# Ten norms of a float32 transformer kernel: the sum of squares as a rounded high and low part

## The chip, the cores and the metric

The kernel runs on one core of a Trainium2 chip. The metric is the device time of one execution in microseconds (us). TensorE is PE in the profile, VectorE is DVE, ScalarE is ACT, GpSimd is POOL. Before the change three runs took 3339.12 to 3342.34 us, with a median of 3340.39 us.

## What is computed

Two blocks of layers, in float32, on 512 tokens of width 1024: feed-forward parts (`swiglu`), mixers (a gated MLP with retention, multi-head attention over latents, a gated linear recurrence) and cross attention to a memory. What matters here is the norm in front of each of them:

```python
def rms_norm(x, g):
    xf = x.astype(jnp.float32)
    y = xf * lax.rsqrt(jnp.mean(xf * xf, axis=-1, keepdims=True) + RMS_EPS)
    return (y * g).astype(x.dtype)
```

The mean of `x*x` over the 1024 features of a token is the sum that the change is about.

## The kernel before

x is held transposed: eight tiles of 128 features by 512 tokens. A product with a weight in near float32 precision is made of three products of rounded parts (type fp32r): high weight by high input, high by low, low by high. A weight unit is 128x1024 (eight tiles of 128x128), so that most units are 24 products of 128x512. There are 588 units; SyncE streams them, ScalarE rounds each to its high part (`whi`, L818), GpSimd subtracts to get the low part (`wlo`, L2182), and TensorE uses them in a fixed order (`unit`, L334 to L346, whose products are L341, L342 and L345).

The work is a chain of twelve stages, 0 to 11: feed-forward at 0, 2, 3, 5, 8 and 11, first mixer at 1 and 4, second mixer at 6, cross attention at 7 and 10, third mixer at 9. A stage ends with `residual`: for each of the eight output tiles m, VectorE adds the product's bank to x (L1472), ScalarE squares x (L849) and rounds x times the gain to `gxh` (L851), VectorE writes the rest to `gxl` (L1480) and adds the square to `acc` (L1483). So `acc`, 128x512, holds the sum of squares over the tiles, and what is left is a sum over the 128 partitions.

That sum is `norm(i)` (L385, by `total`, L381): one matmul of a 128x128 matrix of ones with `acc`, in full float32 precision, into bank 7. In the first product of stage i, TensorE goes through the eight tiles as they arrive; the norm comes right behind this first unit. The gains are in the products' inputs, and the factor 1/rms is only applied behind the products: ScalarE takes the square root (L826, `root`), VectorE the reciprocal (L1359, `rstd`, into R), and VectorE multiplies the banks by R. At stage 9 the unit is taken apart: `high` (16 products), then the norm, then `low` (8 products). Stages 0, 6 and the last norm have orders of their own.

Each engine works through its list in order. On VectorE the last instructions of a residual are, for tile 7, `gxl` and then `acc`; behind them comes the reciprocal of the next stage, which waits for ScalarE. On ScalarE the order there is `gxh`, then the rounding of a weight unit (L818), then the root. On GpSimd there is only the subtraction of the weight units, each as soon as its `whi` is there.

Of the kernel before, what the change touches and what calls it, by code (L numbers as in the profile page):

```python
# [6 lines left out]
F32 = mybir.dt.float32  # L7
F32R = mybir.dt.float32r
I32 = mybir.dt.int32
ALU = mybir.AluOpType  # L10
# [3 lines left out]
P = 128  # L14
SEQ = 512
D = 1024
KD = D // P
# [30 lines left out]
M2_STAGE = 6  # L48
XA_STAGE = (7, 10)
M3_STAGE = 9  # L50
F_SCALE = (0.5, 0.5, 0.5, 0.5, 1.0, 1.0)


# [90 lines left out]
class Signals:  # L144


    def __init__(self, nc, ctx, known):
        self.nc, self.ctx, self.known = nc, ctx, known
        self.handles, self.counts, self.values = {}, {}, {}
# [16 lines left out]
class Memory:  # L166


    def __init__(self, nc, ctx):
        self.nc = nc  # L170
        self.stack = ctx
        sb = self.sb
        self.x = sb("x", KD * SEQ)
        self.gxh, self.gxl = sb("gxh", KD * SEQ, F32R), sb("gxl", KD * SEQ, F32R)
        self.raw = [sb(f"raw{r}", UNIT) for r in range(SLOTS)]
        self.whi = [sb(f"whi{r}", UNIT, F32R) for r in range(SLOTS)]
        self.wlo = [sb(f"wlo{r}", UNIT, F32R) for r in range(SLOTS)]
        self.R, self.acc = sb("R", SEQ), sb("acc", SEQ)
        self.sq, self.xs, self.sd = sb("sq", SEQ), sb("xs", SEQ), sb("sd", SEQ)
        self.ones, self.ident = sb("ones", P, side="right"), sb("ident", P, side="right")  # L180
        self.epsilons, self.later = sb("epsilons", P, side="right"), sb("later", P, side="right")
        self.lcols = [sb(f"lcol{l}", LCOL["all"], side="right") for l in range(DEPTH)]
        self.rcol = sb("rcol", RCOL["all"], side="right")
        self.blocks, self.causal = sb("blocks", P, side="right"), sb("causal", P, side="right")
        self.bank = [ctx.enter_context(nc.psum_tensor(f"bank{n}", [P, 512], F32)) for n in range(8)]
        self.f = [self.ffn_tiles(f) for f in range(6)]
        self.squares = [self.acc, self.sq, self.xs, self.sd, self.R, self.f[0]["a"], self.f[0]["s"], self.f[0]["u"]]
        self.m1 = [self.mixer1_tiles(l) for l in range(DEPTH)]
        self.m2 = self.mixer2_tiles()
        self.xa = [self.memory_tiles(a) for a in range(2)]  # L190
        self.m3 = self.mixer3_tiles()

    def sb(self, name, cols, dt=F32, side="left"):
        return self.stack.enter_context(self.nc.sbuf_tensor(name, [P, cols], dt, side=side))
# [107 lines left out]
def tensor_program(pe, S, M):  # L302
# [78 lines left out]
    def total(emptied, of, n=SEQ):  # L381
        b = claim(7, *emptied)
        return pe.matmul(b[:, 0:n], M.ones[:, :], of, start=True, stop=True)  # L383

    def norm(i):  # L385
        pe.wait_ge(*S.at("acc", i - 1, KD - 1))
        total(("root", i), M.acc[:, :]).then_inc(*S.tick("sum", i))

# [353 lines left out]
    def mixer3():  # L742
# [21 lines left out]
        b = next_bank("xp", 0)  # L764
        high(("m3x", 0), b[:, :], [("gx", M3_STAGE - 1, k) for k in range(KD)])
        norm(M3_STAGE)
        low(("m3x", 0), b[:, :])
# [16 lines left out]
        for m in range(X_EARLY):  # L784
            banks.append(next_bank("xs", M3_STAGE, m))
            part(("o3", m), banks[m][:, :], pairs, range(0, 6), True, False, arrive if m == 0 else None)
        for m in range(X_EARLY):
            part(("o3", m), banks[m][:, :], pairs, range(6, KD), False, True, arrive if m == 0 else None)
        for m in range(X_EARLY, KD):
            unit(("o3", m), next_bank("xs", M3_STAGE, m)[:, :], pairs)  # L790

# [16 lines left out]
def scalar_program(act, S, M, T_in):  # L808
# [11 lines left out]
    def ahead(key):  # L820
        split_hi(U[key] + AHEAD)
# [6 lines left out]
    def residual(i, keys):  # L828
        per, gain = len(keys) // KD, gain_after(M, i)
        if i == M3_STAGE - 1:  # L830
            act.wait_ge(*S.at("hidden", 4, KF - 1))
# [4 lines left out]
        for m in range(KD):  # L836
            for j in range(per):
                if keys[m * per + j]:
                    ahead(keys[m * per + j])
            if i == M3_STAGE - 1 and m == 2:  # L840
                act.wait_ge(*S.at("lam", "ready"))
# [509 lines left out]
def vector_program(dve, S, M):  # L1351
# [9 lines left out]
    def used(*key):  # L1361
        return S.at("used", U[key])
# [77 lines left out]
    def residual(i, last, scale):  # L1440
        gain = gain_after(M, i)
        dve.wait_ge(*(S.at("y2", KD - 1) if i == M2_STAGE else S.at("sum", i)))
        dve.memset(M.acc[:, :], 0.0).then_inc(*S.tick("acc", i, -1))
        if i == M2_STAGE - 1:
            dve.wait_ge(*S.at("hidden", 3, KF - 1))
            dve.memset(M.R[:, :], 0.0).then_inc(*S.tick("acc2", -1))
        for m in range(KD):
            if i == M2_STAGE and m:
                scale_x(m)
            if i == M2_STAGE - 1 and m == 1:  # L1450
                rope_angles()
            if i == M3_STAGE - 1 and m == 1:
                decay_bounds()
            if i == M3_STAGE - 1 and m == 3:
                decay_rates()
            if i == M3_STAGE - 1 and m == 4:
                reset_positions()
            if i == M2_STAGE - 1 and m == 4:
                dve.wait_ge(*S.at("sin", "rsin"))
                dve.tensor_scalar(M.m2["rsin"][:, :], M.m2["rsin"][:, :], M.rc("sign"), None, ALU.mult).then_inc(  # L1460
                    *S.tick("rope_table"))
            dve.wait_ge(*used(*last(m)))
            dve.wait_ge(*S.at("acc", i, m - 1))
            if i == M2_STAGE - 1:
                dve.wait_ge(*S.at("acc2", m - 1))
            if i == M2_STAGE:
                dve.wait_ge(*S.at("x_scaled", m))
            elif i:
                dve.wait_ge(*S.at("xs", i - 1, m))
            else:  # L1470
                dve.wait_ge(*S.at(f"x_tile{m}"))
            dve.scalar_tensor_tensor(seq(M.x, m), at_bank("xs", i, m)[:, :], scale, seq(M.x, m), ALU.mult,  # L1472
                                     ALU.add).then_inc(*S.tick("xs", i, m))
            if i == F_STAGE[5]:
                if m < KD - 1:
                    dve.wait_ge(*S.at("sq", i, m))
                    dve.tensor_tensor(M.acc[:, :], M.acc[:, :], M.sq[:, :], ALU.add).then_inc(*S.tick("acc", i, m))
                continue
            dve.wait_ge(*S.at("gxh", i, m))
            dve.scalar_tensor_tensor(seq(M.gxl, m), seq(M.x, m), gain(m), seq(M.gxh, m).bitcast(F32), ALU.mult,  # L1480
                                     ALU.subtract).then_inc(*S.tick("gx", i, m))
            dve.wait_ge(*S.at("sq", i, m))
            dve.tensor_tensor(M.acc[:, :], M.acc[:, :], M.sq[:, :], ALU.add).then_inc(*S.tick("acc", i, m))  # L1483
            if i == M2_STAGE - 1:
                dve.wait_ge(*S.at("acc2", m - 1))
                dve.wait_ge(*S.at("sq2", m))
                dve.tensor_tensor(M.R[:, :], M.R[:, :], M.sd[:, :], ALU.add).then_inc(*S.tick("acc2", m))
# [14 lines left out]
    def ffn(f):  # L1502
        i, T = F_STAGE[f], M.f[f]
        for m in range(KF):
# [8 lines left out]
            if m:  # L1513
# [9 lines left out]
                *S.tick("hidden", f, m))  # L1523
        residual(i, lambda m: ("down", f, m, 2), F_SCALE[f])

# [635 lines left out]


def pool_program(pool, S, M):
    for name, t in (("ones", M.ones), ("blocks", M.blocks), ("causal", M.causal)):
        pool.memset(t[:, :], 1.0).then_inc(*S.tick("fill", name))
    pool.memset(M.ident[:, :], 0.0).then_inc(*S.tick("fill", "ident"))
    pool.wait_ge(*S.at("fill", "ident"))
    pool.affine_select(out=M.ident[:, :], in_=M.ident[:, :], compare_op=ALU.not_equal, fill=1.0, base=0,
                       pattern=[[-1, P]], channel_multiplier=1).then_inc(*S.tick("masks", "ident"))
    pool.memset(M.epsilons[:, :], EPS).then_inc(*S.tick("fill", "epsilons"))  # L2170
    pool.memset(M.later[:, :], 0.0).then_inc(*S.tick("fill", "later"))
    pool.wait_ge(*S.at("fill", "later"))
    pool.affine_select(out=M.later[:, :], in_=M.later[:, :], compare_op=ALU.is_ge, fill=NEG, base=0,
                       pattern=[[-1, P]], channel_multiplier=1).then_inc(*S.tick("masks", "later"))
    pool.affine_select(out=M.causal[:, :], in_=M.causal[:, :], compare_op=ALU.is_ge, fill=0.0, base=0,
                       pattern=[[1, P]], channel_multiplier=-1).then_inc(*S.tick("masks", "causal"))
    for u in range(NU):
        if u in BY_VECTOR:
            continue
        r = u % SLOTS  # L2180
        pool.wait_ge(*S.at("hi", u))
        pool.tensor_tensor(M.wlo[r][:, :], M.raw[r][:, :], M.whi[r][:, :].bitcast(F32), ALU.subtract).then_inc(  # L2182
            *S.tick("lo", u))
# [157 lines left out]
```

## Time and profile before

| | us |
|---|---|
| median of three runs | 3340.39 |
| the profiled execution | 3341.62 |
| its span | 3340.3 |
| TensorE busy in matmuls | 3268.9 (98%) |
| VectorE busy | 1586.5 (47%) |
| GpSimd busy | 1412.4 (42%) |
| ScalarE busy | 1034.6 (31%) |

The span runs from the first to the last instruction of the program; 1.3 us of the execution lie around it. The profile has a page for the whole execution, and views: a timeline (instructions in order, with the idle time before each and what ended it), the groups by line, the source view of one line, and windows (busy time of each engine in a stretch, and the clock that TensorE was granted, as a share of 2.4 GHz). The ends of matmuls are modelled, so that neighbouring ones overlap in the timeline; how fast TensorE goes is read from start to start. A float32 matmul shows as two MATMUL records, so one norm is two rows of L383, which the timeline may merge into one with x2.

### The profile page before, as it was taken

How to read it: one execution, taken by the hardware profiler on the slowest of the kernel's cores; microseconds unless marked ns; L12 is line 12 of the kernel's file. 1: busy time of each engine (PE TensorE's matmuls, PEld its weight loads, DVE VectorE, ACT ScalarE, POOL GpSimd, SP SyncE). 2: the span in 40 equal slices, each digit the busy share in tenths (PEclk: the TensorE clock that was granted, in tenths of full speed). 3: DMA queues.
4: the chain of work that ended last, by engine and by line, in shares of the span. 5: the costliest groups of instructions: out<-in, count | busy, mean ns of one | idle time of the engine just before them, and what ended most of it. 6: DMA issues, size and time to landing. Idle time of an engine off the chain costs nothing.

```text
span 3340.3 us, 36010 instructions
## 1 busy us (share of the span) xinstructions
PE 3268.9 (98%) x14666; PEld 2673.8 (80%) x14666; DVE 1586.5 (47%) x1826; ACT 1034.6 (31%) x1336; POOL 1412.4 (42%) x583
## 2 busy tenths in 40 slices
PE   8999999999999999999999998999999999999998
PEld 6888877888888888778888866878888878888887
DVE  6441366544134422674454276445444585454421
ACT  3222333322222223323222344333223473332221
POOL 4444433544444444335444422444444205444443
PEclk9999999999999999999999999999999999999999
DMA  4223322322233233223233221323223223222222
GB/s 143 98 96 100 125 76 76 101 97 99 95 108 101 95 100 118 83 76 101 95 101 104 95 63 64 107 83 107 96 95 103 97 84 124 93 97 95 95 95 82
DMA packets 92293, 322.59 MB, mean 97 GB/s; under 512 B 10592, under 2 KB 13024, under 8 KB 91872
## 3 DMA queue, kind: packets, MB, share of 16 engines
q1 hardware_dynamic: 85968, 310.50, 28.0%
q10 hardware_dynamic: 6160, 9.79, 0.9%
q8 instruction: 117, 1.92, 0.2%
q14 instruction: 48, 0.39, 0.0%
HBM read 317.10 MB, written 2.10 MB: 96 GB/s over the span
## 4 chain that ended last, share of the span: by engine, by line
PE 90%; DVE 6%; ACT 2%; issue 1%; DMA 0%; ACTq 0%; SPq 0%; DVEq 0%
PE bank L345 28%; PE bank L341 28%; PE bank L342 28%; PE bank L694 1%; PE bank L672 1%; PE bank L326 1%; PE bank L327 1%; PE bank L330 1%; DVE x L1365 1%; PE bank L469 1%; PE bank L463 1%; ACT whi L818 0%; PE bank L383 0%; PE bank L551 0%; DVE m_yl L1532 0%
## 5 line engine op out<-in xcount | busy, mean ns | idle before, releaser
L2182 POOL TENSOR_TENSOR wlo<-raw,whi 128x1024 fp32r<-128x1024 f32 x570 | 1410.4, 2485 | 1902.5 <-ACT whi L818 1902.4
L341 PE MATMUL bank<-gxh,whi 128*128 128x512 f32 x2808 | 1107.7, 394 | 27.4 <-ACT whi L818 17.6
L342 PE MATMUL bank<-gxl,whi 128*128 128x512 f32 x2808 | 1096.2, 390 | 0.0
L818 ACT ACTIVATE whi<-raw 128x1024 fp32r<-128x1024 f32 x588 | 610.4, 1051 | 582.3 <-PE bank L345 552.0
L345 PE MATMUL bank<-gxh,wlo 128*128 128x512 f32 x2808 | 695.3, 390 | 0.0
L341 PEld LDWEIGHTS bank<-gxh,whi 128*128 128x128 f32 x2808 | 529.1, 188 | 145.5 <-issue 25.0
L342 PEld LDWEIGHTS bank<-gxl,whi 128*128 128x128 f32 x2808 | 529.3, 188 | 113.7 <-issue 5.3
L345 PEld LDWEIGHTS bank<-gxh,wlo 128*128 128x128 f32 x2808 | 528.2, 188 | 110.1
L341 PE MATMUL bank<-f_hh,whi 128*128 128x512 f32 x1056 | 410.8, 389 | 0.0
L342 PE MATMUL bank<-f_hl,whi 128*128 128x512 f32 x1056 | 410.8, 389 | 0.0
L1515 DVE TENSOR_TENSOR f_u<-bank,R 128x512 f32<-128x512 f32 x132 | 91.2, 691 | 590.4 <-PE bank L345 590.4
L1472 DVE SCALAR_TENSOR_TENSOR x<-bank,x 128x512 f32<-128x512 f32 x96 | 66.4, 691 | 589.0 <-PE bank L345 569.2
L1520 DVE TENSOR_SCALAR f_hh<-f_u 128x512 fp32r<-128x512 f32 x132 | 324.6, 2459 | 4.5
L880 ACT ACTIVATE f_s<-f_a 128x512 f32<-128x512 f32 x132 | 83.4, 632 | 648.1 <-DVE f_a L1511 648.1
L345 PE MATMUL bank<-f_hh,wlo 128*128 128x512 f32 x1056 | 262.7, 389 | 0.0
L849 ACT ACTIVATE sq<-x 128x512 f32<-128x512 f32 x96 | 60.7, 632 | 627.7 <-DVE x L1472 627.7
L342 PEld LDWEIGHTS bank<-f_hl,whi 128*128 128x128 f32 x1056 | 198.2, 188 | 41.2
L345 PEld LDWEIGHTS bank<-f_hh,wlo 128*128 128x128 f32 x1056 | 198.2, 188 | 41.1
L341 PEld LDWEIGHTS bank<-f_hh,whi 128*128 128x128 f32 x1056 | 198.2, 188 | 41.1
L1511 DVE TENSOR_TENSOR f_a<-bank,R 128x512 f32<-128x512 f32 x132 | 91.1, 691 | 80.9 <-PE bank L345 80.7
L1522 DVE TENSOR_TENSOR f_hl<-f_u,f_hh 128x512 fp32r<-128x512 f32 x132 | 106.0, 803 | 4.6
L1518 DVE TENSOR_TENSOR f_u<-f_u,f_s 128x512 f32<-128x512 f32 x132 | 91.4, 692 | 14.4 <-DVE f_u L1515 0.9
(349 smaller groups left out, 2618.6 us busy)
## 6 DMA issues: line engine op xcount, KB each, us to landing
raw<-stream SPq DMA_DIRECT2D x588, 512.0 KB, 3.3
m_dk<-decay ACTq DMA_DIRECT2D x2, 1024.0 KB, 5.9
xa_mem<-memT ACTq DMA_DIRECT2D x2, 1024.0 KB, 6.1
x<-xT ACTq DMA_DIRECT2D x4, 256.0 KB, 5.1
x<-xT SPq DMA_DIRECT2D x4, 256.0 KB, 6.6
outT<-x ACTq DMA_DIRECT2D x4, 256.0 KB, 2.2
outT<-x SPq DMA_DIRECT2D x4, 256.0 KB, 2.2
m_ct<-cos ACTq DMA_DIRECT2D x2, 256.0 KB, 2.7
```

The source lines that it names most:

```text
L341: pe.matmul(out, seq(hi, k, P), h, start=first and k == 0, stop=False)
L342: pe.matmul(out, seq(hi, k, P), l, start=False, stop=False)
L345: mm = pe.matmul(out, seq(lo, k, P), h, start=False, stop=last and k == len(pairs) - 1)
L818: act.activation(M.whi[r][:, :], M.raw[r][:, :], ACT.Copy).then_inc(*S.tick("hi", u))
L880: act.activation(T["s"][:, :], T["a"][:, :], ACT.Silu).then_inc(*S.tick("silu", f, m))
L1472: dve.scalar_tensor_tensor(seq(M.x, m), at_bank("xs", i, m)[:, :], scale, seq(M.x, m), ALU.mult, ALU.add).then_inc(*S.tick("xs", i, m))
L1511: dve.tensor_tensor(T["a"][:, :], at_bank("a", f, m)[:, :], M.R[:, :], ALU.mult).then_inc(*S.tick("a", f, m))
L1515: dve.tensor_tensor(T["u"][:, :], at_bank("u", f, m)[:, :], M.R[:, :], ALU.mult).then_inc(*S.tick("u", f, m))
L1518: dve.tensor_tensor(T["u"][:, :], T["u"][:, :], T["s"][:, :], ALU.mult).then_inc(*S.tick("t", f, m))
L1520: dve.tensor_scalar(seq(T["hh"], m), T["u"][:, :], 1.0, None, ALU.mult).then_inc(*S.tick("hh", f, m))
L1522: dve.tensor_tensor(seq(T["hl"], m), T["u"][:, :], seq(T["hh"], m).bitcast(F32), ALU.subtract).then_inc(*S.tick("hidden", f, m))
L2182: pool.tensor_tensor(M.wlo[r][:, :], M.raw[r][:, :], M.whi[r][:, :].bitcast(F32), ALU.subtract).then_inc(*S.tick("lo", u))
```

## The change

For ten norms (stages 1 to 5 and 7 to 11) VectorE writes the last addition twice: once into `acc_hi`, rounded to fp32r, and once into `acc` as before. It then waits for both and writes `acc_lo` = `acc` - `acc_hi`, also fp32r. TensorE waits for `acc_lo` and multiplies a rounded matrix of ones with `acc_hi` and with `acc_lo`, into the same bank. `acc_lo` lies where `xs` lies, and `acc_hi` where `sd` lies. GpSimd fills the second matrix of ones at the start.

```diff
--- before.py
+++ after.py
@@ -48,6 +48,8 @@
 M2_STAGE = 6
 XA_STAGE = (7, 10)
 M3_STAGE = 9
+
+IN_PARTS = (1, 2, 3, 4, 5, 7, 8, 9, 10, 11)
 F_SCALE = (0.5, 0.5, 0.5, 0.5, 1.0, 1.0)
 
 
@@ -176,7 +178,11 @@
         self.whi = [sb(f"whi{r}", UNIT, F32R) for r in range(SLOTS)]
         self.wlo = [sb(f"wlo{r}", UNIT, F32R) for r in range(SLOTS)]
         self.R, self.acc = sb("R", SEQ), sb("acc", SEQ)
-        self.sq, self.xs, self.sd = sb("sq", SEQ), sb("xs", SEQ), sb("sd", SEQ)
+        self.sq = sb("sq", SEQ)
+        parts = self.scoped("sum", [("lo", SEQ, F32R), ("hi", SEQ, F32R)])
+        self.acc_lo, self.acc_hi = parts["lo"], parts["hi"]
+        self.xs, self.sd = sb("xs", SEQ), sb("sd", SEQ)
+        self.rounded_ones = sb("rounded_ones", P, F32R, side="right")
         self.ones, self.ident = sb("ones", P, side="right"), sb("ident", P, side="right")
         self.epsilons, self.later = sb("epsilons", P, side="right"), sb("later", P, side="right")
         self.lcols = [sb(f"lcol{l}", LCOL["all"], side="right") for l in range(DEPTH)]
@@ -383,6 +389,13 @@
         return pe.matmul(b[:, 0:n], M.ones[:, :], of, start=True, stop=True)
 
     def norm(i):
+        if i in IN_PARTS:
+            b = claim(7, "root", i)
+            pe.wait_ge(*S.at("fill", "rounded_ones"))
+            pe.wait_ge(*S.at("acc_lo", i))
+            pe.matmul(b[:, :], M.rounded_ones[:, :], M.acc_hi[:, :], start=True, stop=False)
+            pe.matmul(b[:, :], M.rounded_ones[:, :], M.acc_lo[:, :], start=False, stop=True).then_inc(*S.tick("sum", i))
+            return
         pe.wait_ge(*S.at("acc", i - 1, KD - 1))
         total(("root", i), M.acc[:, :]).then_inc(*S.tick("sum", i))
 
@@ -1480,7 +1493,14 @@
             dve.scalar_tensor_tensor(seq(M.gxl, m), seq(M.x, m), gain(m), seq(M.gxh, m).bitcast(F32), ALU.mult,
                                      ALU.subtract).then_inc(*S.tick("gx", i, m))
             dve.wait_ge(*S.at("sq", i, m))
+            if m == KD - 1 and i + 1 in IN_PARTS:
+                dve.tensor_tensor(M.acc_hi[:, :], M.acc[:, :], M.sq[:, :], ALU.add).then_inc(*S.tick("acc_hi", i + 1))
             dve.tensor_tensor(M.acc[:, :], M.acc[:, :], M.sq[:, :], ALU.add).then_inc(*S.tick("acc", i, m))
+            if m == KD - 1 and i + 1 in IN_PARTS:
+                dve.wait_ge(*S.at("acc_hi", i + 1))
+                dve.wait_ge(*S.at("acc", i, m))
+                dve.tensor_tensor(M.acc_lo[:, :], M.acc[:, :], M.acc_hi[:, :].bitcast(F32), ALU.subtract).then_inc(
+                    *S.tick("acc_lo", i + 1))
             if i == M2_STAGE - 1:
                 dve.wait_ge(*S.at("acc2", m - 1))
                 dve.wait_ge(*S.at("sq2", m))
@@ -2161,7 +2181,7 @@
 
 
 def pool_program(pool, S, M):
-    for name, t in (("ones", M.ones), ("blocks", M.blocks), ("causal", M.causal)):
+    for name, t in (("ones", M.ones), ("rounded_ones", M.rounded_ones.bitcast(F32)), ("blocks", M.blocks), ("causal", M.causal)):
         pool.memset(t[:, :], 1.0).then_inc(*S.tick("fill", name))
     pool.memset(M.ident[:, :], 0.0).then_inc(*S.tick("fill", "ident"))
     pool.wait_ge(*S.at("fill", "ident"))
```

## Rows read from the trace of the kernel before

**Rows 1.** The page, part 4: the chain that ended last, by engine.

```profile
PE 90%; DVE 6%; ACT 2%; issue 1%; DMA 0%; ACTq 0%; SPq 0%; DVEq 0%
```

**Rows 2.** Timeline of TensorE, stage 3: start us, us, instruction, x number of records.

```profile
961.83 0.84 PE L345 MATMUL bank<-gxh,wlo 128*128 128x512 f32 x3
962.52 1.02 PE L383 MATMUL bank<-acc,ones 128*128 128x512 f32 x2
...
963.60 0.40 PE L342 MATMUL bank<-gxl,whi 128*128 128x512 f32 x1
```

**Rows 3.** Timelines of VectorE and GpSimd, stage 3 (in brackets: idle before, releaser).

```profile
959.94 0.68 DVE L1483 TENSOR_TENSOR acc<-acc,sq 128x512 f32<-128x512 f32 x1
...
960.26 2.61 POOL L2182 TENSOR_TENSOR wlo<-raw,whi 128x1024 fp32r<-128x1024 f32 x1 [7.63 <-ACT whi L818]
965.20 2.40 POOL L2182 TENSOR_TENSOR wlo<-raw,whi 128x1024 fp32r<-128x1024 f32 x1 [2.33 <-ACT whi L818]
```

**Rows 4.** Timelines of VectorE and GpSimd, residual of stage 6.

```profile
2084.21 0.68 DVE L1483 TENSOR_TENSOR acc<-acc,sq 128x512 f32<-128x512 f32 x1
2084.81 2.83 DVE L1365 SCALAR_TENSOR_TENSOR x<-x,rcol,R 128x512 f32<-128x512 f32 x1
2087.78 0.69 DVE L1472 SCALAR_TENSOR_TENSOR x<-bank,x 128x512 f32<-128x512 f32 x1
...
2084.53 2.56 POOL L2182 TENSOR_TENSOR wlo<-raw,whi 128x1024 fp32r<-128x1024 f32 x1 [3.68 <-ACT whi L818]
```

**Rows 5.** Source view of L1365: count, min/median/max ns.

```profile
L1365 DVE SCALAR_TENSOR_TENSOR x<-x,rcol,R x8: 743/2885/2895, 2032.3 to 2084.8; 128x512 f32<-128x512 f32 x8
```

**Rows 6.** Timelines of VectorE and TensorE, start of stage 6.

```profile
1901.64 0.68 DVE L1487 TENSOR_TENSOR R<-R,sd 128x512 f32<-128x512 f32 x1
...
1902.43 0.67 PE L504 MATMUL bank<-R,ones 128*128 128x512 f32 x1 [0.46 <-issue]
```

**Rows 7.** Timelines of GpSimd and TensorE, stages 2 and 11.

```profile
600.29 2.61 POOL L2182 TENSOR_TENSOR wlo<-raw,whi 128x1024 fp32r<-128x1024 f32 x1 [2.83 <-ACT whi L818]
...
602.59 1.02 PE L383 MATMUL bank<-acc,ones 128*128 128x512 f32 x2
...
2969.01 2.61 POOL L2182 TENSOR_TENSOR wlo<-raw,whi 128x1024 fp32r<-128x1024 f32 x1 [2.83 <-ACT whi L818]
...
2971.31 1.02 PE L383 MATMUL bank<-acc,ones 128*128 128x512 f32 x2
```

**Rows 8.** Timelines of VectorE, TensorE and GpSimd, stage 1.

```profile
378.66 0.68 DVE L1483 TENSOR_TENSOR acc<-acc,sq 128x512 f32<-128x512 f32 x1
...
381.28 1.02 PE L383 MATMUL bank<-acc,ones 128*128 128x512 f32 x2
...
382.29 2.40 POOL L2182 TENSOR_TENSOR wlo<-raw,whi 128x1024 fp32r<-128x1024 f32 x1 [10.93 <-ACT whi L818]
```

**Rows 9.** Timelines of GpSimd and TensorE, stage 7.

```profile
2090.77 2.59 POOL L2182 TENSOR_TENSOR wlo<-raw,whi 128x1024 fp32r<-128x1024 f32 x1 [3.68 <-ACT whi L818]
...
2095.02 1.28 PE L383 MATMUL bank<-acc,ones 128*128 128x512 f32 x2
```

**Rows 10.** Timelines of VectorE and TensorE, stage 9.

```profile
2628.39 0.68 DVE L1483 TENSOR_TENSOR acc<-acc,sq 128x512 f32<-128x512 f32 x1
...
2629.15 1.10 PE L383 MATMUL bank<-acc,ones 128*128 128x512 f32 x2
```

**Rows 11.** Timeline of TensorE after two pauses.

```profile
514.41 0.67 PE L443 MATMUL bank<-m_rsq,ones 128*128 128x512 f32 x1 [1.54 <-ACT m_rsq L930]
...
1938.28 0.56 PE L371 MATMUL bank<-m_yh,whi 128*128 128x512 f32 x1 [1.95 <-DVE m_K L1716]
1938.63 0.63 PE L372 MATMUL bank<-m_yl,whi 128*128 128x512 f32 x1
```

**Rows 12.** Windows after them: us, busy of each engine, PEclk (granted clock), DMA share, GB/s.

```profile
514.40:518.40 4.00, 3.57 (x33) 2.84 (x35) 0.01 (x1) 3.99 (x6) 0.23 (x1) 1.00 0.00 0
...
1938.30:1942.30 4.00, 4.00 (x11) 3.14 (x12) 3.83 (x10) 0.00 (x0) 0.00 (x0) 0.57 0.41 100
```

## Prediction

> **What bounds the kernel now.** I read the page's chain of waits first: TensorE holds 90% of the chain that ended last [rows 1]. So a time counts here if it lengthens or shortens the row of products on TensorE. Next I read the timelines around the ten norms, on all engines, because the change puts new work between the last addition of the squares and the norm. In the reader's rows the start-to-start time of a product is (962.52 - 961.83) / 3 = 0.23 us, and there is no idle time in front of the norm: it sits between the last product of its unit and the first product of the next one [rows 2]. The last addition into `acc` starts at 959.94 and ends at 960.62, 1.90 us before the norm begins at 962.52 [rows 2, 3]. This is the cover for the added work. The third thing to see is GpSimd: 0.32 us after that addition has started, its subtraction of a weight unit starts, and takes 2.61 us, where the next one takes 2.40 [rows 3].
>
> **The norm on TensorE.** Before: from the start of the norm to the start of the second product behind it are 963.60 - 962.52 = 1.08 us, in which one ordinary product of 0.23 stands [rows 2]. After: two fp32r products and that one, 3 x 0.23 = 0.69, if TensorE doesn't wait. A norm whose parts are ready in time saves 0.39 us. If TensorE has to wait, its first product after the pause takes longer: 1938.63 - 1938.28 = 0.35 [rows 11], and the norm saves 1.08 - 0.35 - 0.23 - 0.23 = 0.27.
>
> The page "TensorE: Matmul & The Clock Gate" of the Trainium skill, section Back-to-back issue gap, gives 131 ns a product for a long stream of load and multiply at 512 columns. The trace doesn't agree (0.23 us in rows 2); by that figure the two products of each norm would take 0.20 us less, ten times, and the sum below would be 2.0 smaller. The row decides.
>
> **The added work on VectorE.** Two additions and a subtraction, 128x512, in place of one addition. An addition takes 0.68 [rows 3]. I take the rounded ones at that too; only their output type differs. Two independent ones start 0.60 apart: 2084.81 - 2084.21 [rows 4]. The subtraction waits for the addition. The trace has no such pair with these two waits; the nearest is L1472 behind L1365: from 2084.81 + 2.83 = 2087.64 to 2087.78, 0.14 [rows 4]. It could be near nothing, so 0 to 0.14 are the ends; I take 0.14. From the end of a VectorE result to the start of the matmul that waits for it: 1901.64 + 0.68 = 1902.32, to 1902.43, 0.11 [rows 6]. Undisturbed, the norm can begin 0.60 + 0.68 + 0.14 + 0.68 + 0.11 = 2.21 us after the start of the first addition. At stage 3 that would be 962.15, before 962.52: hidden.
>
> **But the second addition meets GpSimd.** In the residual of stage 6 the trace shows what an operation of VectorE with two inputs in SBUF does that comes 0.60 behind `acc`, when a weight subtraction has begun on GpSimd in between: L1365 starts at 2084.81 and takes 2.83, to 2087.64, and GpSimd's operation ends at 2084.53 + 2.56 = 2087.09, 0.55 earlier [rows 4]. The undisturbed one takes 0.743, the median of the eight is 2.885 [rows 5]. It was held until GpSimd had finished. The change puts an operation of just that kind at just that place: `acc` = `acc` + `sq`, 0.60 behind `acc_hi`, with GpSimd's start 0.32 behind it. GpSimd's own operation I leave where it is, since `acc_hi` stands where `acc` stood.
>
> The page "SBUF — State Buffer" of the Trainium skill, section Who interferes with whom, says that a VectorE instruction with two SBUF inputs and a GpSimd one that reads SBUF exclude each other, and that the later one waits for the whole of the first. By that GpSimd would begin its 2.40 only at 960.62, and end at 963.02 and not at 962.87; the sum would be 6 x 0.15 = 0.9 larger. The row has 2.61 in all, so I take the row.
>
> So at stage 3: GpSimd ends at 960.26 + 2.61 = 962.87; `acc` at +0.55, `acc_lo` at +0.14 + 0.68, TensorE at +0.11, together 1.48: 964.35. The norm began at 962.52: it comes 1.83 later. Stage 2: 602.90 + 1.48 - 602.59 = 1.79; stage 11: 2971.62 + 1.48 - 2971.31 = 1.79 [rows 7]. Stages 5, 8 and 10 show the same pattern. Six stages at 1.80 are 10.8, less 6 x 0.27 = 1.6: **+9.2**.
>
> Stages 1 and 4: GpSimd's next start is at 382.29, long after the addition at 378.66, because ScalarE issues DMAs first. Ready at 380.87, norm at 381.28 [rows 8]: hidden with 0.4 to spare. Stage 7: GpSimd ends at 2093.36, ready at 2094.84, norm at 2095.02 [rows 9]: just hidden, since TensorE runs slowly there; if it is not, 0.2 us. Three norms save 0.39: **-1.2**.
>
> Stage 9: no GpSimd work, but the norm stands right behind the sixteen high products and begins at 2629.15. Ready at 2628.39 + 2.21 = 2630.60: 1.45 late, less 0.27: **+1.2** [rows 10].
>
> **What else moves.** GpSimd fills one more matrix in its start, under the first loads: nothing. On TensorE the whole list stands behind the new wait. The root on ScalarE and the reciprocal on VectorE start from the norm and move with it; the weight unit that ScalarE rounds behind the root is used two units later, over 10 us, so it isn't late. On VectorE only the reciprocal is behind `acc_lo`, and that waits for the norm anyway. The waits of TensorE in the later parts end with chains that start from the same norm, so I expect none to take the delay back.
>
> **Sum.** 9.2 - 1.2 + 1.2 = +9.2. The profiled execution took 3341.62 (span 3340.3): 3350.8. It stands 1.2 above the median of the three runs, so I forecast 3340.39 + 9.2 = **3349.6**. With the wait on VectorE at nothing it would be 7 x 0.14 = 1.0 less.
>
> **Rivals.** First, *not slower*: the second addition gets through before GpSimd. Then everything is ready 2.21 behind the first addition, nine norms save 0.39 (-3.5), stage 9 stays at +1.2: -2.3, 3338.1. It decides if GpSimd's start falls behind VectorE's second start, 0.60 after the first, or if VectorE is given the port although GpSimd waits. For it: GpSimd's operation begins inside `acc`, so it too has to wait for a while, and may lose its turn. Against it: in rows 4 it had the same 0.32 and the same 0.60, and VectorE lost; the median of rows 5 says that this was the rule. 8 in 100.
>
> Second, *the clock falls in the new pauses*. TensorE will be idle for some 1.80 + 0.23 - 0.40 = 1.6 us at six stages. After a pause of 1.95 the granted clock over 4.00 us was 0.57, after one of 1.54 it was 1.00 [rows 11, 12]. 1.6 is nearer the one that kept it. A fall costs (1 - 0.57) x 4.00 = 1.7 us; six cost 10.3, 3359.9; three, 3354.7. Three or more: 15 in 100. One or two belong to my own case.
>
> Third, *part of the delay is taken back* at a later wait of TensorE that other work ends (10% of the chain is not TensorE, rows 1). If two of the six stages give back their 1.5 us: +6.1, 3346.5. 5 in 100.
>
> **Numbers.** My case has 72 in 100, with its own range 3347.5 to 3353. The range for 8 in 10 takes in the third rival and some of the second: 3346 to 3356. A measurement can tell about 0.2% from no change here, 6.7 us: slower means above 3347.1, faster below 3333.7. Slower: most of my case (68) and the clock (15), 83. Faster: 2, set aside from the first rival's 8 in case it gives more than I see. Same: 15, which is the rest of mine (4), the third (5) and of the first the other 6.
>
> **What would show it.** In the changed kernel the timeline of VectorE must show the second addition at about 3.0 us at stages 2, 3, 5, 7, 8, 10 and 11 and at 0.68 at 1, 4 and 9; TensorE idle about 1.6 us before the norm at six stages and about 1.1 at stage 9, ended by `acc_lo`; L383's norms replaced by two products 0.23 to 0.35 apart. If the second addition takes 0.68 everywhere, the mechanism is wrong and the time should be near 3338. If the time is above 3354, look at the granted clock behind the pauses. The prediction is wrong altogether if TensorE waits as foreseen and the span doesn't grow.

## The result, and the profile after

The changed kernel took 3348.97 us in the median of 11 runs (3348.11 to 3350.85), the kernel before 3340.94 us (3335.86 to 3343.16, 11 runs). The ratio is 1.0026, with a 95% interval of 1.0018 to 1.0034: slower by 8.0 us, where +9.2 was forecast. The profiled execution took 3348.11 us, its span is 3346.9.

In the profile after, line numbers have moved: the last additions are L1497 (into `acc_hi`, which the trace calls `sum_hi`) and L1498 (into `acc`), the subtraction is L1502 (`sum_lo`), and the two products of the norm are L396 and L397. The page, parts 1 and 4, answers to [rows 1]:

```profile
PE 3263.6 (98%) x14666; PEld 2671.3 (80%) x14666; DVE 1613.2 (48%) x1846; ACT 1034.5 (31%) x1336; POOL 1414.0 (42%) x584
...
PE 89%; DVE 7%; ACT 2%; issue 1%; DMA 0%; ACTq 0%; SPq 0%; DVEq 0%
PE bank L351 27%; PE bank L347 27%; PE bank L348 27%; PE bank L707 1%; DVE acc L1498 1%; PE bank L685 1%; PE bank L332 1%; PE bank L333 1%; PE bank L336 1%; DVE x L1378 1%; PE bank L482 1%; PE bank L476 1%; ACT whi L831 0%; DVE x L1485 0%; 
```

TensorE's share of the chain is 1% less, VectorE's 1% more, and the last addition, L1498, which was not among the lines of the chain, has 1% of the span by itself. The totals hide how that comes; stage 3 shows it. These are the timelines of VectorE, GpSimd and TensorE there, to be laid beside [rows 2, 3]:

```profile
959.98 0.69 DVE L1497 TENSOR_TENSOR sum_hi<-acc,sq 128x512 fp32r<-128x512 f32 x1
960.58 2.88 DVE L1498 TENSOR_TENSOR acc<-acc,sq 128x512 f32<-128x512 f32 x1
963.57 0.69 DVE L1502 TENSOR_TENSOR sum_lo<-acc,sum_hi 128x512 fp32r<-128x512 f32 x1
...
960.30 2.62 POOL L2202 TENSOR_TENSOR wlo<-raw,whi 128x1024 fp32r<-128x1024 f32 x1 [7.63 <-ACT whi L831]
...
964.41 0.47 PE L396 MATMUL bank<-sum_hi,rounded_ones 128*128 128x512 f32 x1 [1.69 <-DVE sum_lo L1502]
964.72 0.40 PE L397 MATMUL bank<-sum_lo,rounded_ones 128*128 128x512 f32 x1
964.95 0.39 PE L347 MATMUL bank<-gxh,whi 128*128 128x512 f32 x1
965.18 0.39 PE L348 MATMUL bank<-gxl,whi 128*128 128x512 f32 x1
```

The first addition takes 0.69 us. GpSimd starts 0.32 us behind its start, as before. The second addition comes 0.60 behind the first, takes 2.88 instead of 0.68, and ends at 963.46, 0.54 after GpSimd at 962.92. The subtraction ends at 964.26, and at 964.41 TensorE begins the norm, after a pause of 1.69 us that `sum_lo` ended. The second product behind the norm is at 965.18, where it was at 963.60.

How often: the source view of L1498, and the row of the waits that has the norm.

```profile
L1498 DVE TENSOR_TENSOR acc<-acc,sq x88: 681/684/2887, 272.9 to 2974.0; 128x512 f32<-128x512 f32 x88
...
PE bank L396 <- DVE sum_lo L1502: 11.4, 7, 1.7
```

The shortest and the middle one of the 88 additions are as before, the longest is 2887 ns (687 before). TensorE waits for `sum_lo` seven times, 11.4 us in all: the six stages and stage 9. Stage 9 and stage 7 by themselves:

```profile
2632.71 0.68 DVE L1498 TENSOR_TENSOR acc<-acc,sq 128x512 f32<-128x512 f32 x1
2633.50 0.69 DVE L1502 TENSOR_TENSOR sum_lo<-acc,sum_hi 128x512 fp32r<-128x512 f32 x1
...
2634.34 0.47 PE L396 MATMUL bank<-sum_hi,rounded_ones 128*128 128x512 f32 x1 [1.30 <-DVE sum_lo L1502]
...
2095.27 0.69 DVE L1502 TENSOR_TENSOR sum_lo<-acc,sum_hi 128x512 fp32r<-128x512 f32 x1
...
2096.28 0.63 PE L396 MATMUL bank<-sum_hi,rounded_ones 128*128 128x512 f32 x1
```

At stage 9 nothing holds the addition (0.68 us), and still TensorE pauses for 1.30 us. The second product behind the norm of stage 9, in the kernel before and in the changed one:

```profile
2630.32 0.39 PE L363 MATMUL bank<-gxh,wlo 128*128 128x512 f32 x1
...
2635.11 0.39 PE L369 MATMUL bank<-gxh,wlo 128*128 128x512 f32 x1
```

At stage 7 `sum_lo` ends at 2095.96 and the norm begins at 2096.28, without idle time.

TensorE has the same number of matmuls in both kernels (14666), in the same order. So the start of each can be compared with the start of its counterpart, and the difference can be read off on both sides of every norm. What it grows by there (from 18 matmuls before the norm to 34 behind it; at stage 9 from 3 before), in us:

| stage | 1 | 2 | 3 | 4 | 5 | 7 | 8 | 9 | 10 | 11 | sum |
|---|---|---|---|---|---|---|---|---|---|---|---|
| forecast | -0.39 | +1.5 | +1.6 | -0.39 | +1.5 | -0.39 | +1.5 | +1.2 | +1.5 | +1.5 | +9.2 |
| measured | -0.41 | +1.49 | +1.53 | -0.32 | +1.54 | -0.42 | +1.44 | +1.03 | +1.53 | +1.53 | +8.9 |

It also moves away from the norms. It is -1.0 at the very first matmul already: ScalarE rounds the first weight unit at 10.28 us and not at 11.29, since the load of that unit, for which it waits, landed earlier. In the six other changed kernels the first matmul is 0.07 to 1.08 earlier than in the one profiled execution of the kernel before, so this differs from run to run; whether the change has a part in it is not shown. Then the difference goes by -1.5, +1.5 and -1.5 in the attention parts (behind 2026, 2208 and 2820 us of the kernel before). Here are the windows of both kernels for the last of these, behind the same pause of TensorE (2.4 us, at 2815.7 in the kernel before). The granted clock has two levels, 2.4 and 1.2 GHz, which show as 1.00 and 0.50 of full speed; a figure in between is the mean of a window with both. In the kernel before it is 0.57,

```profile
2815.70:2819.70 4.00, 3.98 (x21) 4.00 (x22) 3.21 (x4) 0.00 (x0) 3.81 (x2) 0.57 0.38 119
```

and in the changed kernel (second row below) it is 1.00. The first row is the window behind the new pause at stage 3, with the clock at 1.00 too; the other five are the same.

```profile
964.40:968.40 4.00, 3.99 (x18) 3.32 (x19) 2.62 (x1) 2.83 (x3) 1.62 (x1) 1.00 0.25 99
...
2821.90:2825.90 4.00, 3.95 (x33) 3.98 (x34) 3.68 (x5) 0.75 (x2) 3.90 (x2) 1.00 0.35 123
```

So these two executions differ by steps of 1.5 us according to which of the old pauses the clock falls behind. -1.0 + 8.9 - 1.5 + 1.5 - 1.5 = +6.4; the starts of the last matmuls differ by 6.5. The medians, over eleven executions each, differ by 8.0.

### The profile page after: what moved, and what is told of

Same layout as the page of the kernel before. It is cut to its first block, busy times and chain, and to the rows that moved or that the text cites. A ratio compares the mean times of both kernels' runs of the same rounds, so it can differ in the third digit from the quotient of the medians.

```text
span 3346.9 us, 36041 instructions
## 1 busy us (share of the span) xinstructions
PE 3263.6 (98%) x14666; PEld 2671.3 (80%) x14666; DVE 1613.2 (48%) x1846; ACT 1034.5 (31%) x1336; POOL 1414.0 (42%) x584
## 4 chain that ended last, share of the span: by engine, by line
PE 89%; DVE 7%; ACT 2%; issue 1%; DMA 0%; ACTq 0%; SPq 0%; DVEq 0%
PE bank L351 27%; PE bank L347 27%; PE bank L348 27%; PE bank L707 1%; DVE acc L1498 1%; PE bank L685 1%; PE bank L332 1%; PE bank L333 1%; PE bank L336 1%; DVE x L1378 1%; PE bank L482 1%; PE bank L476 1%; ACT whi L831 0%; DVE x L1485 0%; ACT gxh L864 0%
```

## The experiments

Theory: at seven stages the second addition is held until GpSimd's weight subtraction ends; six of these make TensorE wait, and stage 9 waits because its norm has no products in front. Rivals: the chain of three VectorE operations is too long by itself; the rounded products are no cheaper; the clock falls behind the new pauses. The first four kernels ran beside the kernel before on one chip (3342.36 us there, 27 runs), the last two on another occasion (3340.4 us, 15 runs).

**GpSimd waits.** The held operation is set free without touching VectorE or TensorE:

```diff
+FIRST = {2: ("gate", 1, 0), 3: ("gate", 2, 0), 5: ("gate", 3, 0), 7: ("xq", 0, 0, 0), 8: ("gate", 4, 0),
+         10: ("xq", 1, 0, 0), 11: ("gate", 5, 0)}
+BEHIND_SUM = {U[key] + AHEAD: i for i, key in FIRST.items()}
...
         pool.wait_ge(*S.at("hi", u))
+        if u in BEHIND_SUM:
+            pool.wait_ge(*S.at("acc_lo", BEHIND_SUM[u]))
```

> The changed kernel, in which GpSimd waits for acc_lo before it subtracts the weight unit that it would begin inside the last addition (seven stages: 2, 3, 5, 7, 8, 10, 11). It touches no instruction of VectorE or TensorE. Theory (the second addition is held until GpSimd's subtraction ends): the second addition takes 0.68 everywhere, the norm is ready 2.2 us after the first addition begins, the pause before it is gone at the six stages, each of which goes from +1.5 to -0.4 against the kernel before; stage 9 keeps its +1.0. Time 3340.9 - 9 x 0.39 + 1.0 = 3338.4, 0.9968 of the changed kernel. Rival (three operations that wait for one another are simply too long a chain, and GpSimd has no part in it): no change, 3349. Rival (the weight unit that GpSimd now finishes 1.9 us later is late on TensorE): 3349 or more.

Measured: 3338.53 us, ratio 0.9990 (0.9981 to 0.9998). The timelines of VectorE, GpSimd and TensorE at stage 3:

```profile
958.30 0.69 DVE L1502 TENSOR_TENSOR sum_hi<-acc,sq 128x512 fp32r<-128x512 f32 x1
958.90 0.68 DVE L1503 TENSOR_TENSOR acc<-acc,sq 128x512 f32<-128x512 f32 x1
959.69 0.69 DVE L1507 TENSOR_TENSOR sum_lo<-acc,sum_hi 128x512 fp32r<-128x512 f32 x1
...
960.52 2.41 POOL L2209 TENSOR_TENSOR wlo<-raw,whi 128x1024 fp32r<-128x1024 f32 x1 [9.53 <-DVE sum_lo L1507]
...
960.43 0.62 PE L356 MATMUL bank<-gxh,wlo 128*128 128x512 f32 x2
960.88 0.39 PE L401 MATMUL bank<-sum_hi,rounded_ones 128*128 128x512 f32 x1
961.12 0.39 PE L402 MATMUL bank<-sum_lo,rounded_ones 128*128 128x512 f32 x1
961.34 0.40 PE L352 MATMUL bank<-gxh,whi 128*128 128x512 f32 x1
961.58 0.40 PE L353 MATMUL bank<-gxl,whi 128*128 128x512 f32 x1
```

The second addition takes 0.68 us, the third operation ends at 960.38, GpSimd starts behind it, and the norm follows the last product at 0.23 us without a pause: from its start to the second product behind it are 961.58 - 960.88 = 0.70 us, against 1.08 in [rows 2]. At all seven stages the second addition now takes 0.68 or 0.69. The loss is gone with nothing but GpSimd's turn changed, so the length of the chain alone was not the cause at these six stages. GpSimd's unit, begun 1.9 us later, is late for nobody: the six stages go by -0.32 to -0.42 against the kernel before, and from one stage to the next the starts grow by no more than 0.05. Stage 9 keeps its pause of 1.3 us. That the time is so near the 3338.4 of the forecast is luck in part, since on this chip the kernel before took 1.4 us more than the 3340.9 it was counted from; the ratio that the forecast implies, 0.9993, lies inside the interval.

**TensorE's part alone.**

```diff
-            pe.wait_ge(*S.at("acc_lo", i))
+            pe.wait_ge(*S.at("acc_hi", i))
...
-            pe.matmul(b[:, :], M.rounded_ones[:, :], M.acc_lo[:, :], start=False, stop=True).then_inc(*S.tick("sum", i))
+            pe.matmul(b[:, :], M.rounded_ones[:, :], M.acc_hi[:, :], start=False, stop=True).then_inc(*S.tick("sum", i))
```

The subtraction on VectorE and its two waits are left out too.

> TensorE's part alone: VectorE writes acc_hi and acc, but no acc_lo, and TensorE multiplies the rounded ones twice with acc_hi, so that the low part is left out of the ten sums and the high part counts double. It waits for the first addition only. Theory (two rounded products cost 0.39 us less than one full one, and all of the loss is the wait): no pause anywhere, 10 x -0.39 against the kernel before: 3337.0. The second addition is still held to about 2.9 us at seven stages, and nobody waits for it. Rival (the products save nothing, and the pause costs less than it seems): 3341. Rival (the additions on VectorE cost by themselves, as through GpSimd or through later stages): above 3341.

Measured: 3338.53 us, ratio 0.9989 (0.9980 to 0.9998); 3342.36 - 3.9 = 3338.5 was to be expected on this chip. VectorE and TensorE at stage 3:

```profile
959.65 0.69 DVE L1497 TENSOR_TENSOR sum_hi<-acc,sq 128x512 fp32r<-128x512 f32 x1
960.25 2.89 DVE L1498 TENSOR_TENSOR acc<-acc,sq 128x512 f32<-128x512 f32 x1
...
961.78 0.62 PE L351 MATMUL bank<-gxh,wlo 128*128 128x512 f32 x2
962.23 0.39 PE L396 MATMUL bank<-sum_hi,rounded_ones 128*128 128x512 f32 x1
962.47 0.39 PE L397 MATMUL bank<-sum_hi,rounded_ones 128*128 128x512 f32 x1
```

The second addition is held for 2.89 us here as well, and it costs nothing, for nobody waits for it. What the change saves on TensorE is real: nine stages go by -0.33 to -0.42 each. (Stage 7 goes by -1.36 here and by -1.32 in the kernel in which GpSimd waits. In both the clock had risen to its full level when the norm began; in the kernel before, the same unit ran at 0.50 up to the norm.)

**One more operation in the chain.**

```diff
-                dve.tensor_tensor(M.acc_lo[:, :], M.acc[:, :], M.acc_hi[:, :].bitcast(F32), ALU.subtract).then_inc(
+                dve.tensor_tensor(M.sq[:, :], M.acc[:, :], M.acc[:, :], ALU.max).then_inc(*S.tick("again", i + 1))
+                dve.wait_ge(*S.at("again", i + 1))
+                dve.tensor_tensor(M.acc_lo[:, :], M.sq[:, :], M.acc_hi[:, :].bitcast(F32), ALU.subtract).then_inc(
```

> The changed kernel with one more VectorE operation of 128x512 between the second addition and acc_lo (it copies acc into sq by a maximum of acc with itself). Theory (TensorE waits for the end of this chain, and each 0.1 us in it counts): the operation and its wait are 0.72 to 0.83 us; it counts in full at the six stages and at stage 9 (7 x 0.8 = 5.6), in part at stages 1 and 4, where 0.4 was to spare (2 x 0.4), and at stage 7 (0.6): 3349 + 7 = 3356, if the clock keeps its level. The pauses grow from 1.68 to about 2.45. The clock rival: at that length the granted clock falls behind some of them, as it did after pauses of 1.9 to 2.4 elsewhere, at about 1.6 us each: up to 3366. If the chain doesn't set the wait: 3349.

Measured: 3361.4 us (3357.14 to 3363.51, 5 runs), ratio 1.0062 (1.0048 to 1.0076). By the medians that is 19.0 us over the kernel before, where 15 was forecast if the clock keeps its level, and up to 25 if it falls. The profiled execution is the fastest of them. The source view of the norm's first product, the start of the norm at stage 9, and the windows behind the pauses at stages 2 and 9:

```profile
L396 PE MATMUL bank<-sum_hi,rounded_ones x10: 467/472/476, 380.6 to 2986.6; 128*128 128x512 f32 x10
...
2639.51 0.47 PE L396 MATMUL bank<-sum_hi,rounded_ones 128*128 128x512 f32 x1 [2.02 <-DVE sum_lo L1504]
...
604.20:608.20 4.00, 4.00 (x18) 3.33 (x19) 2.67 (x1) 2.83 (x3) 1.68 (x1) 1.00 0.11 43
...
2639.50:2643.50 4.00, 3.99 (x12) 3.19 (x13) 2.62 (x1) 1.54 (x2) 0.00 (x0) 0.67 0.00 0
```

The norm now starts from idle at all ten stages (its shortest record is 467 ns; 392 in the changed kernel). The five stages 2, 3, 5, 8 and 11 grow by 2.17 to 2.29 us each, 0.7 more than in the changed kernel, which is the added operation. At stage 9, behind a pause of 2.02 us, the clock falls to 0.67 over 4.00 us; at stage 10, behind 2.41, it does too, and these stages grow by 3.39 and 3.85, each 1.6 more than in the changed kernel plus the 0.7. Behind the other five pauses of 2.4 it stays at 1.00. So a longer pause can cost more than its length, but not each time. Whether the other executions, up to 6.4 us slower, have more such falls is open: they have no trace.

**Both mends.** As the first, and at stage 9:

```diff
-        norm(M3_STAGE)
         low(("m3x", 0), b[:, :])
+        norm(M3_STAGE)
```

> As the one in which GpSimd waits for acc_lo, and at stage 9 the norm comes behind the eight low products instead of in front of them. Theory: the stage's wait of 1.3 us lies beside 8 x 0.23 = 1.8 us of products and goes, all ten norms save 0.39: 3340.9 - 3.9 = 3337.0, 1.4 less than with the GpSimd wait alone, and below both kernels. Rival (at stage 9 root and reciprocal, 1.8 us of products later, hold up the first bank that VectorE has to read): no gain against the GpSimd wait alone, 3338.4.

Measured: 3338.27 us (3335.15 to 3340.72), ratio 0.9988 (0.9979 to 0.9997). VectorE and TensorE at stage 9:

```profile
2626.83 0.69 DVE L1507 TENSOR_TENSOR sum_lo<-acc,sum_hi 128x512 fp32r<-128x512 f32 x1
...
2627.57 0.62 PE L374 MATMUL bank<-gxh,wlo 128*128 128x512 f32 x2
2628.02 0.39 PE L401 MATMUL bank<-sum_hi,rounded_ones 128*128 128x512 f32 x1
```

`sum_lo` ends at 2627.52, half a microsecond before its turn, and the pause is gone: stage 9 grows by -0.48 where it grew by +1.03, and all ten stages are between -0.20 and -0.48. These 1.5 us show in the trace; in the times the two kernels (0.9990 and 0.9988) can't be told apart. Both intervals end just below 1, and well below that of the changed kernel (1.0018 to 1.0034).

**The norm one unit later.** The change untouched on VectorE and GpSimd, and the norm of five feed-forward stages behind their second unit:

```diff
-            if m == 0 and f:
-                norm(i)
             project(("up", f, m), next_bank("u", f, m)[:, :])
-            if m == 0 and not f:
+            if m == 0:
                 norm(i)
```

> The changed kernel, in which the norm of the feed-forward stages 2, 3, 5, 8 and 11 comes one unit later on TensorE, behind the first up product (5.4 us of products) instead of in front of it. VectorE and GpSimd do the same as in the changed kernel, the second addition is still held. Theory: the chain is as long as before but now lies beside products, so that these five stages go from +1.5 to -0.4; stages 1, 4 and 7 stay at -0.4, stage 10 at +1.5 and stage 9 at +1.0: -0.7 against the kernel before, ratio 0.9998. Rival (being held costs by itself, wherever the norm stands, or root and reciprocal come too late for the banks): 1.002 or more.

Measured: 3342.84 us, ratio 1.0005 (0.9997 to 1.0014). The forecast 0.9998 lies inside the interval, the rival's 1.002 outside. VectorE and TensorE at stage 2:

```profile
599.06 2.88 DVE L1496 TENSOR_TENSOR acc<-acc,sq 128x512 f32<-128x512 f32 x1
602.05 0.69 DVE L1500 TENSOR_TENSOR sum_lo<-acc,sum_hi 128x512 fp32r<-128x512 f32 x1
...
606.03 0.62 PE L351 MATMUL bank<-gxh,wlo 128*128 128x512 f32 x2
606.48 0.39 PE L396 MATMUL bank<-sum_hi,rounded_ones 128*128 128x512 f32 x1
```

The addition is held for 2.88 us as in the changed kernel, but its result is there at 602.74 and needed at 606.48. The five stages go by -0.32 to -0.45, stages 9 and 10 by +1.07 and +1.49, and all ten together by -0.4, near the -0.7 of the forecast. The medians differ by +2.4. In the profiled execution the largest other part is a step of +1.5 between stages 7 and 8, where the granted clock fell to 0.60 behind an old pause of 2.5 us and kept 1.00 in the kernel before. So it is not the holding that costs, but the holding with too few products in front of the norm.

**VectorE's part alone.** TensorE makes the old product, and waits for the new work:

```diff
-        if i in IN_PARTS:
...
-            return
-        pe.wait_ge(*S.at("acc", i - 1, KD - 1))
+        pe.wait_ge(*(S.at("acc_lo", i) if i in IN_PARTS else S.at("acc", i - 1, KD - 1)))
         total(("root", i), M.acc[:, :]).then_inc(*S.tick("sum", i))
```

> VectorE's part alone: acc_hi and acc_lo are written as in the change, and TensorE makes the norm as before, one full-precision product of ones with acc, but waits for acc_lo. Theory: the pause is as in the changed kernel (1.7 us at six stages, 1.3 at stage 9) and nothing is saved on the norm: the changed kernel plus 10 x 0.39, or the kernel before plus 6 x 1.9 + 1.5 = 12.9, ratio 1.0039. Rival (the rounded products start later than a full one would, and are part of the loss): no more than the changed kernel, ratio 1.0026 or less.

Measured: 3352.8 us, ratio 1.0040 (1.0026 to 1.0054), where 1.0039 was forecast. The rival's 1.0026 is the lower end of the interval; what decides against it is the trace. TensorE at stage 3:

```profile
965.12 1.12 PE L389 MATMUL bank<-acc,ones 128*128 128x512 f32 x2 [1.60 <-DVE sum_lo L1495]
965.68 0.79 PE L347 MATMUL bank<-gxh,whi 128*128 128x512 f32 x1
966.32 0.39 PE L348 MATMUL bank<-gxl,whi 128*128 128x512 f32 x1
```

The pause is 1.60 us, and the norm takes 966.32 - 965.12 = 1.20 us to the second product behind it, where the rounded pair takes 965.18 - 964.41 = 0.77 in the changed kernel. The six stages grow by 1.81 to 1.87 us instead of 1.44 to 1.54. The parts add up, by the medians: +12.4 us for the wait alone, -3.8 for the cheaper norm alone, together +8.6; both at once are the change, +8.0. Each of these is uncertain by several us (the interval of the first alone is 8.7 to 18.0), so that the sum agrees so well is luck in part; the stages in the traces carry the argument.

## Why the prediction was right

- *The norm alone saves 0.39 where its parts are ready.* Measured 0.41, 0.32 and 0.42 at stages 1, 4 and 7, and 0.32 to 0.48 at nearly all ten when nothing waits. From a pause it was put at 0.81 us to the second product behind; it took 0.77, since the first product after the pause took 0.31 and not 0.35.
- *The second addition is held until GpSimd ends, at seven stages, not at 1, 4 and 9.* So it was: 2.85 to 2.89 us, and 0.68 at the three. The pattern was to be had from one pair of operations of another line that stood in the same order and distance [rows 4]. The experiment with GpSimd shows that this is the cause.
- *Ready 1.48 us after GpSimd's end.* Measured 964.41 - 962.92 = 1.49. Its parts were less exact: the wait on VectorE took 0.11 and not 0.14, the way to TensorE 0.15 and not 0.11. They cancel.
- *Stage 7 just hidden, stages 1 and 4 with room.* Measured: 0.3 us to spare at stage 7, where 0.18 was forecast.
- *Stage 9: +1.2.* Measured +1.03. The chain was as foreseen; its wait on VectorE took 0.11 us (2633.39 to 2633.50). The saving was taken from stage 3, and at stage 9 it is larger, because the old norm was dearer there: 2630.32 - 2629.15 = 1.17 us to the second product behind it, against 1.08 at stage 3. The rounded pair takes 2635.11 - 2634.34 = 0.77 there, so the norm saves 0.40 and not 0.27, and 1.45 - 0.40 is +1.05.
- *The rounded products at 0.23 us.* Where nothing waits they are 0.23 to 0.24 us apart (960.88, 961.12, 961.34 in the kernel in which GpSimd waits). The Trainium skill ("TensorE: Matmul & The Clock Gate", Back-to-back issue gap) would have given 0.13 and a sum of 7.2. That is as near to the measured +8.0 as 9.2 is, so the time can't judge between the two; the trace does.
- *GpSimd's operation stays at 2.61.* Measured 2.62. Excluded from the whole of the first addition, as the Trainium skill has it ("SBUF — State Buffer", Who interferes with whom), it would have shown 0.68 - 0.32 + 2.40 = 2.76. That the second addition, the later one, ends only 0.54 us behind GpSimd's end agrees with the same section.
- *The clock keeps its level behind 1.6 us.* The pauses were 1.65 to 1.69 us, and the clock stayed at 1.00 behind all six in the profiled execution. With 2.0 to 2.4 us, in the kernel with one more operation, it fell behind two of seven. The rival was close.
- *Nothing is taken back.* The difference stays behind each stage until the end, but for the steps of the clock behind old pauses, which go both ways.

The forecast +9.2 is above the +8.0 of the medians. The stages measured in the trace give +8.9; the rest is smaller than one step of 1.5 us by the clock behind an old pause, but that such steps are the reason is not shown. The absolute 3349.6 is nearer to its 3348.97 than the difference is, which is luck: it was counted from the median of three runs, 3340.39, and eleven gave 3340.94.

## What to carry to other kernels

Work added behind the last operation of a chain can be exposed even where the time in front of its user looks long enough: undisturbed, the parts of stage 3 would have been ready at 962.15, before the norm at 962.52. Look at what the *other* engine starts while the old last operation runs, since the next one may have to wait for all of it, as VectorE's did for GpSimd's 2.6 us. A pair of operations with the same order and distance elsewhere in the trace gives the price. Such a wait on the bounding engine was mended here in two ways that leave the work as it is: more products in front of the norm, and a later start of the other engine.

## What the runs showed of the hardware

- A VectorE addition of 128x512 with two SBUF inputs (0.68 us alone) that comes 0.28 us after a GpSimd subtraction of 128x1024 has started ends 0.54 to 0.55 us after that subtraction's end, 2.85 to 2.89 us after its own start, seven times out of seven. It does not get its turn in between, though GpSimd's subtraction, which started 0.32 us into the VectorE operation before, is itself lengthened (2.62 us in place of 2.40). In both orders the one that is held ends 0.14 us earlier than if it began only at the end of the other: 0.68 - 0.54, and 0.68 - 0.32 + 2.40 - 2.62.
- The granted clock behind pauses of about the same length is not the same: of the seven new pauses of 2.0 to 2.4 us in the kernel with one more operation two brought it down, and one old pause of 2.4 us brought it down in the kernel before (0.57) and not in the changed one (1.00). A fall costs 1.5 to 1.6 us. Each kernel has one trace, so none of them shows two executions of one kernel; but the 27 executions of the kernel before, on one chip, spread from 3337.21 to 3343.87, and the six fastest have a mean granted clock of 0.994 or 0.995, the other 21 of 0.992 or 0.993. That fits steps in the time that no edit caused.
